# Two convolution chunks as one seven-product block, and half of the depthwise taps shared by ScalarE and VectorE

## The chip, the cores and the metric

The kernel runs on one core of a Trainium2 chip. The metric is the device time of one execution in microseconds (us). The engines are TensorE (PE, matmuls), VectorE (DVE), ScalarE (ACT), GpSimd (POOL) and SyncE (SP, which issues most transfers). Each has its own in-order instruction queue, and they synchronise by semaphores.

## The reference, cut to what matters

One decoder layer on x of 256 x 2048, in float32: a SwiGLU feed-forward part (FFN), a token mixer, a second FFN, each with a normalisation behind it. The mixer:

```python
z = h @ w_in                      # 2048 x 12288
q, k, v, u, ga, gc = split(z)     # widths 2048, 2048, 2048, 2*1024, 2048, 2048
y_attn = attention(q, k, v) @ w_attn_out
a, g = jnp.split(u, 2, axis=-1)
c = a * jax.nn.sigmoid(g)                          # 256 x 1024
c = depthwise_causal_conv(c, w_dw, 31 taps) + b_dw # per channel
y_conv = silu(layer_norm(c)) @ w_conv_out
mix = (sigmoid(ga) * y_attn + sigmoid(gc) * y_conv) @ w_out
```

## The kernel before, in words

**Arithmetic.** Each float32 matmul is made of three faster ones: activations and weights are each split into a high part (fp32r) and a low part, and high x high, high x low and low x high are added up. ScalarE writes the high part of a weight tile (`g_hi`, `w_hi`), VectorE the low part by a subtraction (`g_lo`, `w_lo`).

**Groups.** The weights of the FFNs and of `w_in` come as groups of 512 rows x 512 columns (1 MB). A group is loaded by SP into one of up to eight slots of `g_raw`, split into a ring of four (`RING`), and used by TensorE. The class `Groups` numbers groups in the order in which TensorE uses them and gives each load a slot; SP issues a load when the low part of the slot's last user is made. ScalarE's split of group n waits until TensorE has used group n-4.

**Plain and seven-product work.** The 256 rows are two tiles of 128. A plain group is used for both tiles: 24 matmuls of 512 columns. A plain chunk of 512 output columns is four groups. A seven-product block computes two chunks at once (Winograd's form of Strassen's scheme over 2 x 2 blocks of rows and inner dimension): products P1 to P7, each in two half groups a and b, so 14 product groups of 12 matmuls. Some of its weight groups are sums of loaded ones: VectorE adds them in place (T1a, T2a, T2b and so on, `add`), or a POOL transfer accumulates a group from memory onto a slot (`add_from_hbm`). Between products ScalarE copies PSUM banks (`fork`, `save_value`).

**The order of the mixing stage.** Four plain chunks for the convolution input u (gate and value of the first 512 channels, then of the second), with 33 taps of the depthwise convolution on VectorE near their end; then six `mixing_block`s, each a seven-product block for two chunks (keys and values, or gates) with four plain query groups Q1 to Q4 among it (the last for queries or a gate); attention heads of block g-1 are worked on inside block g. Then eight plain gate groups, here called gates 0 to 7. Then `attn_out`, four chunks of eight units. A unit is 256 rows x 512 columns (512 KB) with 6 matmuls for each row tile; TensorE goes through four units for the first row tile, then the same four for the second. The units come through four slots of `raw` and eight split slots (`SPLIT`). The conv and output projections follow.

**Taps.** The convolution's rows are kept transposed in `ch`, eight tiles of 128 channels x (30 + 256) positions. `taps(count)` does the next `count` steps of 248 (8 tiles x 31 taps), each a multiply-add of 128 x 256 on VectorE into `cacc`, two tiles in turn. Their places are written out by hand: 33 before the mixing blocks, 97 in them (`BLOCK_TAPS`), 8 or 6 behind each gate's low part, then 3 behind each unit's low part in `attn_out`. The second turn of the finished rows (`turn_conv_out(1)`) is behind unit 3 of the third chunk. In the last four gates VectorE also makes `oT_lo`, the low part of four attention heads, after ScalarE's `heads_hi`; the heads come back from memory (`oT`, loaded by SP behind the load of gate 3).

ScalarE's order at the gates, in which these names matter, is: split gate 0, a sigmoid of a bank, split gate 1, a sigmoid, split gate 2, two sigmoids of the banks of Q4, split gate 3, two sigmoids of `sig_c`, `heads_hi(0)`, then split gates 4 to 7 with the other `heads_hi`, with `gate_out(0)` before the split of gate 7; then the splits of units 0 to 3, `gate_out(1)`, and the other units.

## Time and profile before

| | |
|---|---|
| median of 3 runs | 2111.5 us (2111.37 to 2112.41) |
| profiled execution, first to last instruction (its span) | 2109.5 us |
| TensorE busy | 2095.7 us, 99% |
| VectorE busy | 1877.2 us, 89% |
| ScalarE busy | 1402.9 us, 67% |
| mean granted TensorE clock | 0.998 |

For the profiled execution only the span is recorded; the median of the runs lies 2.0 us above it. The span runs from the first to the last instruction, so what lies around it (start and end of the execution) is in the runs' times alone. In the rows below, a timeline row gives start, duration, engine, source line, operation, tiles and count, and in brackets the idle time before it and what ended it. A matmul's shown duration is longer than the distance from one to the next.

### The profile page before, as it was taken

What the parts mean: (1) busy time and instruction counts of PE and PEld (TensorE: products, weight loads), DVE (VectorE), ACT (ScalarE), POOL (GpSimd) and SP (SyncE); (2) the same over time, 40 slices, a digit from 0 to 9 for tenths busy, and PEclk for the clock granted to TensorE, in tenths of its full rate; (3) what the DMA queues carried; (4) which work ended last, traced back from release to release, by engine and by line L of the source; (5) the groups of instructions that cost most, each with busy time, mean ns of one, the idle gap of its engine ahead of it and who ended that gap; (6) DMA issues with size and microseconds to landing.
All of it is one profiled execution on the core that took longest, in us unless ns stands there. A gap on an engine that the chain in (4) does not pass through costs nothing.

```text
span 2109.5 us, 23778 instructions
## 1 busy us (share of the span) xinstructions
PE 2095.7 (99%) x9386; PEld 1734.6 (82%) x9386; DVE 1877.2 (89%) x1420; ACT 1402.9 (67%) x1313; POOL 216.7 (10%) x345
## 2 busy tenths in 40 slices
PE   9999999999999999999999999999999999999998
PEld 7888888888888888888888888888888888888886
DVE  7899999999996889999999986659899999999996
ACT  6677777777775546766676445335677777777773
POOL 0111111101110001011100000000111111100110
PEclk9999999999999999999999999999999999999999
DMA  9798988888985759998898556755788988899892
GB/s 369 253 295 260 279 270 266 291 300 277 289 279 231 276 158 311 299 269 270 304 301 262 212 185 240 260 178 200 244 294 255 282 272 267 290 302 278 288 285 113
DMA packets 92397, 556.65 MB, mean 264 GB/s; under 512 B 13056, under 2 KB 13440, under 8 KB 35200
## 3 DMA queue, kind: packets, MB, share of 16 engines
q1 hardware_dynamic: 68544, 437.69, 54.7%
q0 software_dynamic: 23744, 117.46, 25.8%
q8 instruction: 74, 1.21, 0.2%
q14 instruction: 35, 0.29, 0.0%
HBM read 534.13 MB, written 20.97 MB: 263 GB/s over the span
## 4 chain that ended last, share of the span: by engine, by line
PE 88%; DVE 8%; DMA 2%; ACT 1%; issue 1%; SPq 0%; DVEq 0%; ACTq 0%
PE acc L2259 14%; PE acc L2261 14%; PE acc L2260 14%; PE tb L2259 12%; PE tb L2261 12%; PE tb L2260 12%; PE acc L2197 3%; PE acc L2199 3%; PE acc L2198 3%; DVE g_lo L1338 3%; DVE cacc L1777 3%; DMA g_raw<-in_groups 1%; PE tb L2245 1%; DVE w_lo L1315 1%; DVE g_raw L1346 1%
## 5 line engine op out<-in xcount | busy, mean ns | idle before, releaser
L1338 DVE TENSOR_TENSOR g_lo<-g_raw,g_hi 128x2048 fp32r<-128x2048 f32 x506 | 1147.6, 2286 | 120.4 <-ACT g_hi L817 119.8
L817 ACT ACTIVATE g_hi<-g_raw 128x2048 fp32r<-128x2048 f32 x506 | 964.4, 1916 | 319.8 <-DVE g_raw L1346 121.5
L2259 PE MATMUL acc<-g_hi,xF_hi 128*128 128x512 f32 x1184 | 464.3, 392 | 0.6 <-ACT acc L899 0.6
L2261 PE MATMUL acc<-g_hi,xF_lo 128*128 128x512 f32 x1184 | 461.1, 389 | 0.0
L2260 PE MATMUL acc<-g_lo,xF_hi 128*128 128x512 f32 x1184 | 460.7, 389 | 0.0
L2259 PE MATMUL tb<-g_hi,xF_hi 128*128 128x512 f32 x760 | 296.3, 390 | 0.3 <-DVE g_lo L1338 0.2
L2261 PE MATMUL tb<-g_hi,xF_lo 128*128 128x512 f32 x760 | 295.7, 389 | 0.0
L2260 PE MATMUL tb<-g_lo,xF_hi 128*128 128x512 f32 x760 | 295.7, 389 | 0.0
L1346 DVE TENSOR_TENSOR g_raw<-g_raw,g_raw 128x2048 f32<-128x2048 f32 x120 | 274.3, 2286 | 1.3
L2259 PEld LDWEIGHTS acc<-g_hi,xF_hi 128*128 128x128 f32 x1184 | 222.3, 188 | 46.8 <-ACT acc L899 1.0
L2261 PEld LDWEIGHTS acc<-g_hi,xF_lo 128*128 128x128 f32 x1184 | 222.2, 188 | 46.8
L2260 PEld LDWEIGHTS acc<-g_lo,xF_hi 128*128 128x128 f32 x1184 | 222.4, 188 | 45.1
L2259 PEld LDWEIGHTS tb<-g_hi,xF_hi 128*128 128x128 f32 x760 | 142.7, 188 | 30.4 <-issue 1.1
L2261 PEld LDWEIGHTS tb<-g_hi,xF_lo 128*128 128x128 f32 x760 | 142.6, 188 | 29.8
L2102 POOL DMA_DIRECT2D g_raw<-in_groups x80 | 72.5, 941 | 918.8 <-DVE g_lo L1338 870.6
L2260 PEld LDWEIGHTS tb<-g_lo,xF_hi 128*128 128x128 f32 x760 | 142.7, 188 | 29.4
L767 ACT ACTIVATE w_hi<-raw 128x1024 fp32r<-128x1024 f32 x80 | 84.7, 1062 | 105.0 <-DMA raw<-in_stream 65.4
L2259 PE MATMUL tb<-g_hi,hT_hi 128*128 128x512 f32 x384 | 149.8, 390 | 0.0
L2261 PE MATMUL tb<-g_hi,hT_lo 128*128 128x512 f32 x384 | 149.4, 389 | 0.0
L2260 PE MATMUL tb<-g_lo,hT_hi 128*128 128x512 f32 x384 | 149.4, 389 | 0.0
L2259 PE MATMUL acc<-g_hi,hT_hi 128*128 128x512 f32 x320 | 124.7, 390 | 0.0
L2261 PE MATMUL acc<-g_hi,hT_lo 128*128 128x512 f32 x320 | 124.5, 389 | 0.0
(180 smaller groups left out, 2307.7 us busy)
## 6 DMA issues: line engine op xcount, KB each, us to landing
g_raw<-in_groups SPq DMA_DIRECT2D x356, 1024.0 KB, 7.2
g_raw<-in_groups POOLq DMA_DIRECT2D x80, 1024.0 KB, 8.6
raw<-in_stream SPq DMA_DIRECT2D x80, 512.0 KB, 4.5
bounce<-h_sq POOLq DMA_DIRECT2D x40, 256.0 KB, 5.5
h_in<-bounce POOLq DMA_DIRECT2D x160, 64.0 KB, 2.6
ln_gb<-in_ln SPq DMA_DIRECT2D x6, 1024.0 KB, 6.6
g_raw<-in_groups SPq DMA_DIRECT2D x6, 512.0 KB, 9.7
res<-in_x_rows SPq DMA_DIRECT2D x1, 2048.0 KB, 16.6
```

Source lines behind the costliest of these rows:

```text
L767: act.activation(w_hi[:, seg.split(j)], raw[:, seg.raw(j)], ACT.Copy).then_inc(hi_ready, 1)
L817: act.activation(g_hi[:, n % RING], source[:], ACT.Copy).then_inc(g_hi_ready, 1)
L1338: dve.tensor_tensor(g_lo[:, n % RING], source[:], f32(g_hi[:, n % RING]), ALU.subtract).then_inc(g_lo_ready, 1)
L1346: dve.tensor_tensor(out[:], a[:], b[:], ALU.add).then_inc(t_ready, 1)
L1777: ins = dve.scalar_tensor_tensor(out=rows if j == TAPS - 1 else cacc[:, k], in0=rows, scalar=w, in1=cacc[:, k], op0=ALU.mult, op1=ALU.add)
L2102: pool.dma_start(out=source(f, b, onto)[:].rearrange("p k n -> p (k n)"), in_=groups[k], accum_op=ALU.add).then_inc(ready, 16)
L2197: pe.matmul(out_ap, x[0][:, k, rows], w_hi[:, s, cols], start=begin, stop=False)
L2198: pe.matmul(out_ap, x[0][:, k, rows], w_lo[:, s, cols], start=False, stop=False)
L2199: return pe.matmul(out_ap, x[1][:, k, rows], w_hi[:, s, cols], start=False, stop=end)
L2259: pe.matmul(bank, x_hi_ap, g_hi[:, n % RING, blk], start=begin, stop=False, skip_group_check=True)
L2260: pe.matmul(bank, x_hi_ap, g_lo[:, n % RING, blk], start=False, stop=False, skip_group_check=True)
L2261: return pe.matmul(bank, x_lo_ap, g_hi[:, n % RING, blk], start=False, stop=end, skip_group_check=True)
```

## The change

The second pair of convolution chunks (value and gate of the second 512 channels), eight plain groups before, becomes a seven-product block of its own (`conv_pair`, numbered as block -1, `CONV`). The first mixing block begins with its query group Q1 (`FIRST_MIXING`), behind which the sigmoids read the pair's results; its product with the value moves to `conv_pair_value`. The loads are reordered to match. The 33 taps before the mixing blocks go. VectorE keeps the 124 taps of four tiles (97 in the mixing blocks as before, 4 behind each gate's low part). For the other four tiles ScalarE makes the products of row and tap (`tap_rounds`: a round is one tap of two tiles, two activations of 128 x 256), and VectorE adds two tiles at once (`shared_taps`: one add of 128 x 512 a round, none in the first round of each pair). There are 62 rounds.

```diff
-SPLIT0 = 2
+SPLIT0 = 6
+FIRST_MIXING = ("Q1", "P1a", "P1b", "Q2") + MIXING[4:]
+FIRST_MIXING_LOADS = ("Q1", "qa", "qb", "ra", "Q2", "ua", "rb", "ub", "Q3", "ga", "gb", "Q4")
+PAIR = ("P1a", "P1b", "P5a", "P5b", "P6a", "P3a", "P6b", "P3b", "P7a", "P7b", "P2a", "P2b", "P4a", "P4b")
+PAIR_LOADS = {"qa": "P4a", "ra": "P7a", "qb": "P4b", "rb": "P7b", "ua": "P3a", "ub": "P3b", "ga": "P2a", "gb": "P2b"}
+PAIR_SUMS = ("T1a", "T1b", "T2a", "T2b")
...
+TAP_ROUNDS = ((0, 1), (2, 3))
+SHARED = ((4, 5), (6, 7))
+OWN_TAPS = sum(TAPS * len(tiles) for tiles in TAP_ROUNDS)
+SHARED_ADDS = (TAPS - 1) * len(SHARED)
... SyncE
-            sp.wait_ge(conv_step, 2 + KC * TAPS)
+            sp.wait_ge(conv_step, 2 + OWN_TAPS)
+            sp.wait_ge(shared_added, SHARED_ADDS)
... ScalarE
+            def conv_pair():
+                f, g = "mix", CONV
+                split_loaded(f, g, "P1a", "qa")
+                split_loaded(f, g, "P1b", "qb")
+                split_sum(f, g, "P5a", "qa", "T1a")
+                split_sum(f, g, "P5b", "qb", "T1b")
+                fork(f, g, acc[:, BY], acc[:, BX], "P1b")
+                split_sum(f, g, "P6a", "qa", "T2a")
+                split_loaded(f, g, "P3a", "ua")
+                split_sum(f, g, "P6b", "qb", "T2b")
+                act.wait_ge(acc_out[1], 2)
+                fork(f, g, acc[:, BZ], acc[:, BW], "P5b")
+                split_loaded(f, g, "P3b", "ub")
+                conv_block(0)
+                act.wait_ge(t3a_ready, 16)
+                split(f, g, "P7a", "ra")
+                act.wait_ge(t3b_ready, fulls(f, g))
+                split(f, g, "P7b", "rb")
+                save_value(g, 0, "P6b")
+                split_loaded(f, g, "P2a", "ga")
+                save_value(g, 1, "P7b")
+                split_loaded(f, g, "P2b", "gb")
+                act.wait_ge(t4a_ready, fulls(f, g))
+                split(f, g, "P4a", "qa")
+                act.wait_ge(t4b_ready, 16)
+                split(f, g, "P4b", "qb")
...
+            def tap_rounds(rounds):
+                for r in range(products_done[0], min(products_done[0] + rounds, TAPS * len(SHARED))):
+                    j, n = r // len(SHARED), r % len(SHARED)
+                    if j == 0:
+                        act.wait_ge(o_stored, 16 * NG)
+                        act.wait_ge(ch_ready, 4)
+                    elif j > 1:
+                        act.wait_ge(shared_added, r - 2 * len(SHARED) + 1)
+                    for k, c in enumerate(SHARED[n]):
+                        w = cw[:, c * TAPS + j:c * TAPS + j + 1]
+                        if j == 0:
+                            act.activation(shared_sum[:, n, k], ch[:, c, j:j + T], ACT.Identity, scale=w,
+                                           bias=cw[:, KC * TAPS + c:KC * TAPS + c + 1]).then_inc(tap_products, 1)
+                        else:
+                            act.activation(shared_product[:, n, k], ch[:, c, j:j + T], ACT.Copy,
+                                           scale=w).then_inc(tap_products, 1)
+                products_done[0] += rounds
...
             heads_hi(0)
+            tap_rounds(6)
             for g in range(PIECES, PIECES * GATES):
                 if g % PIECES == PIECES - 1:
                     gate_out(g // PIECES - 1)
                 split_gate(g)
+                tap_rounds(4)
                 if g in HEADS_AT:
                     heads_hi(HEADS_AT.index(g))
             hi(attn_out, 0, 0, 1, 2, 3)
             gate_out(GATES - 1)
-            hi(attn_out, 0, 4, 5, 6, 7)
-            hi(attn_out, 1, *range(UD))
-            hi(attn_out, 2, *range(UD))
+            for j in range(4, UD):
+                tap_rounds(2)
+                hi(attn_out, 0, j)
... and the same for all units of chunks 1 and 2
... VectorE
+            def shared_taps(rounds):
+                for r in range(shared_done[0], min(shared_done[0] + rounds, TAPS * len(SHARED))):
+                    j, n = r // len(SHARED), r % len(SHARED)
+                    if j == 0:
+                        continue
+                    add_no = r - len(SHARED)
+                    c = SHARED[n][0]
+                    dve.wait_ge(tap_products, 2 * (r + 1))
+                    if add_no > 1:
+                        dve.wait_ge(shared_added, add_no - 1)
+                    dve.tensor_tensor(ch[:, c:c + 2, PAD:PAD + T] if j == TAPS - 1 else shared_sum[:, n], shared_sum[:, n],
+                                      shared_product[:, n], ALU.add).then_inc(shared_added, 1)
+                shared_done[0] += rounds
...
+            def conv_pair():
+                lo_group P1a; add T1a (qa += ra); lo_group P1b; add T1b (qb += rb); lo_group P5a; add T2a (qa += ua)
+                conv_value(0); lo_group P5b; add T2b (qb += ub)
+                lo_group P6a, P3a, P6b, P3b, P7a, P7b, P2a, P2b, P4a; values(g); lo_group P4b
... block 0 of mixing_block on VectorE: lo Q1, lo P1a, conv_pair_value, lo P1b, add T1a, taps, lo Q2 ...
-            lo_conv(8) ... lo_conv(15), conv_value(0), taps(11) three times
+            conv_pair()
             for g in range(PIECES * GATES):
                 lo_gate(g)
-                taps(6 if g - 1 in HEADS_AT else 8)
+                taps(4)
+                shared_taps(2 if g - 1 in HEADS_AT else 3)
                 if g - 1 in HEADS_AT:
... oT_lo of four heads
             for j in range(UD):
                 lo(attn_out, 0, j)
-                taps(3)
+                shared_taps(2)
... and the same in chunk 1 and in four units of chunk 2
... GpSimd
+            def conv_pair_sums():
+                f, g = "mix", CONV
+                pool.wait_ge(t_ready, G.sum_no[f, g, "T1a"])
+                add_from_hbm(f, g, "ra", "ua", t3a_ready)
+                pool.wait_ge(t_ready, G.sum_no[f, g, "T1b"])
+                add_from_hbm(f, g, "rb", "ub", t3b_ready)
+                pool.wait_ge(g_lo_ready, lo_count(G.at[f, g, "P6a"]))
+                add_from_hbm(f, g, "qa", "ga", t4a_ready)
+                pool.wait_ge(g_lo_ready, lo_count(G.at[f, g, "P6b"]))
+                add_from_hbm(f, g, "qb", "gb", t4b_ready)
... TensorE: conv_pair runs PAIR in order, turn_conv(0) behind P5b; block 0 begins with query_group(0, 0),
... then P1a, P1b, turn_conv(1), Q2, P5a, P5b as before
-            plain_chunk(conv + 2 * PIECES, (acc[:, 0], acc[:, 1]), after={(3, 0): lambda: turn_conv(0)})
-            plain_chunk(conv + 3 * PIECES, (acc[:, 2], acc[:, 3]))
+            conv_pair()
```

## Rows read from the trace of the kernel before

**Rows 1.** The page, busy time of each engine over the whole span.
```profile
PE 2095.7 (99%) x9386; PEld 1734.6 (82%) x9386; DVE 1877.2 (89%) x1420; ACT 1402.9 (67%) x1313; POOL 216.7 (10%) x345
```

**Rows 2.** TensorE's waits: us in total, times, longest.
```profile
PE tb L2323 <- DVE zeros L1683: 1.5, 1, 1.5
...
PE acc L2197 <- DVE sig_a L1950: 0.7, 1, 0.7
```

**Rows 3.** Groups by line and shape: busy us, mean ns of one, idle before.
```profile
L1392 DVE TENSOR_TENSOR hT_lo<-h_in,hT_hi 128x512 fp32r<-128x512 f32 x40 | 25.9, 685 | 1.6 <-ACT hT_hi L835 1.6
...
L1117 ACT ACTIVATE pr<-pr,nmax 128x256 f32<-128x256 f32 x16 | 7.9, 495 | 0.0
...
L1124 ACT ACTIVATE pT<-tb 128x384 f32<-128x384 f32 x16 | 6.8, 480 | 0.0
```

**Rows 4.** TensorE's timeline: chunk 2, P3a of block 0, gate 0, attention output.
```profile
723.11 0.39 PE L2259 MATMUL acc<-g_hi,xF_hi 128*128 128x512 f32 x1
...
794.22 0.50 PE L2259 MATMUL acc<-g_hi,xF_hi 128*128 128x512 f32 x1 [0.61 <-ACT acc L899]
...
1157.78 0.39 PE L2259 MATMUL acc<-g_hi,xF_hi 128*128 128x512 f32 x1
...
1201.30 0.39 PE L2197 MATMUL acc<-w_hi,oT_hi 128*128 128x512 f32 x1
```

**Rows 5.** VectorE's timeline in the convolution chunks and block 0.
```profile
714.55 4.49 DVE L1338 TENSOR_TENSOR g_lo<-g_raw,g_hi 128x2048 fp32r<-128x2048 f32 x2
...
746.38 0.73 DVE L1774 TENSOR_SCALAR cacc<-ch,cw 128x256 f32<-128x256 f32 x2 [7.00 <-ACT ch L1077]
...
789.44 2.28 DVE L1346 TENSOR_TENSOR g_raw<-g_raw,g_raw 128x2048 f32<-128x2048 f32 x1
```

**Rows 6.** ScalarE's timeline in block 0, the fork behind P5b.
```profile
793.59 0.58 ACT L899 ACTIVATE acc<-acc 128x512 f32<-128x512 f32 x1
```

**Rows 7.** VectorE's timeline at the gates and the first attention output units.
```profile
1153.06 3.26 DVE L1777 SCALAR_TENSOR_TENSOR cacc<-ch,cw,cacc 128x256 f32<-128x256 f32 x8
1156.23 2.30 DVE L1338 TENSOR_TENSOR g_lo<-g_raw,g_hi 128x2048 fp32r<-128x2048 f32 x1
...
1161.60 2.30 DVE L1338 TENSOR_TENSOR g_lo<-g_raw,g_hi 128x2048 fp32r<-128x2048 f32 x1
...
1176.91 1.24 DVE L1942 TENSOR_TENSOR oT_lo<-oT,oT_hi 128x1024 fp32r<-128x1024 f32 x1
...
1189.47 2.30 DVE L1338 TENSOR_TENSOR g_lo<-g_raw,g_hi 128x2048 fp32r<-128x2048 f32 x1
...
1205.62 1.22 DVE L1315 TENSOR_TENSOR w_lo<-raw,w_hi 128x1024 fp32r<-128x1024 f32 x1
```

**Rows 8.** ScalarE's timeline at the gates.
```profile
1157.98 1.09 ACT L1212 ACTIVATE sig_a<-tb 128x512 f32<-128x512 f32 x2 [2.26 <-PE tb L2261]
1158.95 1.92 ACT L817 ACTIVATE g_hi<-g_raw 128x2048 fp32r<-128x2048 f32 x1
1160.76 1.15 ACT L1249 ACTIVATE sig_c<-sig_c 128x512 f32<-128x512 f32 x2
1163.14 1.06 ACT L1218 ACTIVATE oT_hi<-oT 128x1024 fp32r<-128x1024 f32 x1 [1.23 <-DMA oT<-heads_out]
1165.62 1.92 ACT L817 ACTIVATE g_hi<-g_raw 128x2048 fp32r<-128x2048 f32 x1 [1.42 <-DMA g_raw<-in_groups]
...
1168.94 1.92 ACT L817 ACTIVATE g_hi<-g_raw 128x2048 fp32r<-128x2048 f32 x1 [0.45 <-DMA g_raw<-in_groups]
```

**Rows 9.** ScalarE's timeline, splits of units 0 and 8.
```profile
1195.36 1.06 ACT L767 ACTIVATE w_hi<-raw 128x1024 fp32r<-128x1024 f32 x1 [12.73 <-DMA raw<-in_stream]
...
1214.44 1.06 ACT L767 ACTIVATE w_hi<-raw 128x1024 fp32r<-128x1024 f32 x1 [3.03 <-DMA raw<-in_stream]
```

**Rows 10.** TensorE's timeline at the start of the kernel.
```profile
1.47 4.63 PE L2323 MATMUL tb<-zeros 128*128 128x512 f32 x10 [1.47 <-DVE zeros L1683]
5.90 1.02 PE L2313 MATMUL acc<-g_hi,xF_hi 128*128 128x512 f32 x2
```

More of the change, by code:

```diff
@@ L1134, in save_value, with conv_gate_out @@
                 fork("mix", g, act_sb[:, t], acc[:, BX], behind)
+            def conv_pair():
[24 more added lines that the diff above has]
+                split(f, g, "P4b", "qb")
+            def conv_gate_out(t):
+                act.wait_ge(g_used, mix_used(CONV, ("P2b", "P4b")[t]))
+                act.activation(k_sb[:, t], acc[:, (BY, BX)[t]], ACT.Sigmoid).then_inc(k_out, 1)
             def mixing_block(g):
@@ L1838, in queries_squared, with conv_pair_value @@
                     square(q_sq[:, :, t], act_sb[:, t], q_squared)
+            def conv_pair():
+                f, g = "mix", CONV
+                qa, qb, ra, rb, ua, ub = (source(f, g, name) for name in ("qa", "qb", "ra", "rb", "ua", "ub"))
+                lo_group(f, g, "P1a", "qa")
+                load_done(f, g, "ra")
+                split_done(f, g, "P1a")
+                add(qa, qa, ra)
+                lo_group(f, g, "P1b", "qb")
+                load_done(f, g, "rb")
+                split_done(f, g, "P1b")
+                add(qb, qb, rb)
+                lo_group(f, g, "P5a", "qa")
+                load_done(f, g, "ua")
+                split_done(f, g, "P5a")
+                add(qa, qa, ua)
+                conv_value(0)
+                lo_group(f, g, "P5b", "qb")
+                load_done(f, g, "ub")
+                split_done(f, g, "P5b")
+                add(qb, qb, ub)
+                lo_group(f, g, "P6a", "qa")
+                lo_group(f, g, "P3a", "ua")
+                lo_group(f, g, "P6b", "qb")
+                lo_group(f, g, "P3b", "ub")
+                lo_group(f, g, "P7a", "ra")
+                lo_group(f, g, "P7b", "rb")
+                lo_group(f, g, "P2a", "ga")
+                lo_group(f, g, "P2b", "gb")
+                lo_group(f, g, "P4a", "qa")
+                values(g)
+                lo_group(f, g, "P4b", "qb")
+            def conv_pair_value():
+                dve.wait_ge(k_out, TT)
+                dve.wait_ge(v_out, TT)
+                for t in range(TT):
+                    dve.tensor_tensor(act_sb[:, t], k_sb[:, t], vt[:, t], ALU.mult).then_inc(acc_out[1], 1)
             def mixing_block(g):
@@ L1964, in _ @@
                     attn_rows(1, (j // 2,))
-                taps(3)
+                shared_taps(2)
             for t in range(TT):
@@ L2569, in query_group, with conv_pair @@
                 plain_piece(G.at["mix", g, f"Q{p + 1}"], (tb[:, 2], tb[:, 3]), p)
+            def conv_pair():
+                f, g = "mix", CONV
+                X, Y, Z, W = (acc[:, bank] for bank in (BX, BY, BZ, BW))
+                pe.wait_ge(acc_out[0], 2)
+                product_group(f, g, "P1a", X, A11, 0, begin=True)
+                product_group(f, g, "P1b", X, A11, 1)
+                pe.wait_ge(x_lo, 11 + 4 * factors("mix"))
+                pe.wait_ge(acc_out[1], 2)
+                product_group(f, g, "P5a", W, S1, 0, begin=True)
+                product_group(f, g, "P5b", W, S1, 1)
+                turn_conv(0)
+                wait_fork(f, g, 0)
+                product_group(f, g, "P6a", X, S2, 0)
+                wait_fork(f, g, 1)
+                product_group(f, g, "P3a", Z, S4, 0)
+                product_group(f, g, "P6b", X, S2, 1)
+                product_group(f, g, "P3b", Z, S4, 1)
+                wait_fork(f, g, 2)
+                product_group(f, g, "P7a", X, S3, 0)
+                product_group(f, g, "P7b", X, S3, 1)
+                product_group(f, g, "P2a", Y, A12, 0)
+                product_group(f, g, "P2b", Y, A12, 1)
+                wait_fork(f, g, 3)
+                product_group(f, g, "P4a", X, A22, 0)
+                product_group(f, g, "P4b", X, A22, 1)
             def mixing_block(g):
```

157 lines of the change are left out of this document (88 added, 69 removed).

## The prediction

> **What bounds the kernel now.** I read the engine line of the page first, then TensorE's waits, then the timelines around the two edited stages. TensorE is busy 99% [rows 1], and the view of its waits has nothing longer than 1.5 us. One wait of 0.67 us behind VectorE lies in the attention output [rows 2], one of 0.61 us in block 0 [rows 4]. So only fewer matmuls, or new waits, can move the time. From the first gate matmul at 1157.78 to the first attention output matmul at 1201.30 lie 8 groups of 24 matmuls in 43.52 us [rows 4], so a matmul costs 0.2267 us: a product group (12) 2.72, a plain group (24) 5.44, a unit of the attention output (12) 2.72. Each group also needs a high part from ScalarE (1.92 [rows 8]) and a low part from VectorE (2.29, or 2.20 in a row: 4.49 for two [rows 5]). VectorE comes closest to TensorE: in a gate group it does one low part and 8 taps and starts the next 5.37 us later [rows 7], against TensorE's 5.44. It is however ahead: gate 1's low part ends at 1158.5 and is needed at 1163.2.
>
> **Part 1, the seven products.** They take 14 x 12 = 168 matmuls where the two chunks took 192: 24 x 0.2267 = -5.4 us. For VectorE 33 taps leave this stage (0.40 each in a row, 13.1 us), and 6 low parts and 4 adds come (2.20 each, 22.0). Before, VectorE had holes here, the last of 7.0 us [rows 5], so it must be laid out. Chunk 2 starts at 723.11 [rows 4], the first low part of the pair at 714.55 [rows 5]. From there to the end of block 0's T2b add, VectorE has 21 low parts and 8 adds (29 x 2.20 = 63.8), six 512-column products and subtractions (3.6), 6 taps (2.4) and 0.8 for adds that wait for the low part just issued: 70.6. One wait comes on top. Before P2b, ScalarE first copies the value bank that P7b completes, then splits: P7b's end at 752.5, 0.2 until ScalarE starts (as from 1157.78 to 1157.98 [rows 4, 8]), 0.5 for the copy and 1.95 for the split give 755.2, when VectorE has been free since 749.4: 5.8 of idle. T2b ends at 714.6 + 76.4 = 791.0, or 0.1 later where instructions don't overlap. Before, it ended at 789.44 + 2.28 = 791.7 [rows 5], and behind it came ScalarE's P6b split, the fork at 793.59 [rows 6] and TensorE's P3a at 794.22 [rows 4]. All of this comes 0.6 earlier, and TensorE's 5.4 saved are spent on waits at P5a (0.9: VectorE's conv product), P6a (0.4), P2b (2.3), P4b (0.1), and in block 0 at P5b (0.9) and P3a (1.4, where it was 0.8, and chunk 3 lost 0.3): 6.0 less the 1.1 of before. **Net -0.6.** Bounds: -6.2 (all saved, and the old wait gone too) and +1.5 (POOL's accumulating load for P4b or P5b lands late). The four added POOL loads follow adds and low parts by 15 us or more before their split is due. The moved SP loads wait for low parts at least 10 us ahead of their use, and lie beside that slack. The query group before P1a costs nothing: its 5.44 us of matmuls cover the sigmoids (0.6 each) that read the pair's banks. From block 0's P3a to the gates everything keeps its order, 0.6 earlier.
>
> **Part 2, the gates.** Here VectorE's in-order queue gets a wait it did not have. After gate 0's low part and 4 taps, `shared_taps(3)` skips rounds 0 and 1 and stands at round 2, which needs six tap products. ScalarE makes them only behind the sigmoids of Q4's banks, the split of gate 3, two sigmoids and `heads_hi(0)`, which waits for the DMA of oT: all those rows are in [rows 8]. Behind VectorE's wait stands gate 1's low part, and behind that TensorE. heads_hi started at 1163.14, now 1162.5 (the 0.6). Six products follow from 1163.5.
>
> The trace has no tap product on ScalarE. Nearest are an Exp of 128x256 with a per-partition operand, 0.495, and a copy of 128x384 without one, 0.480 [rows 3]. Less 128 columns, and overlapped by 0.1 as two sigmoids are (1.09 for two of 0.6 [rows 8]), the copy gives 0.28 each in a row, the Exp 0.40; 0.495 is the end above. I take 0.40 with 0.49 for the last, since the products carry such an operand. The Trainium skill (ScalarE: Activation LUTs, What ACT_TABLE_LOAD costs) says that each pointer operand adds about 93 ns to an activation; at 0.28 the whole sum below would be about +15, at 0.40 it is +19.6, and this trace has no pair of rows that isolates the operand.
>
> So the sixth product ends at 1166.0, the shared add (0.69, 0.60 in a row, from the 512-column row in [rows 3]) is over at 1166.6, and gate 1's low part is there at 1168.9. TensorE finished gate 0 at 1157.18 + 5.44 = 1162.6: **6.3 us idle.** Afterwards VectorE's cycle for a group is low part 2.20, 4 taps 1.6, adds 1.2 to 1.8, plus `oT_lo` 1.14 from gate 4 on: 5.6 to 6.1, more than 5.44, with no lead left. Gate 2 waits 0.6 (round 5's products wait for round 3's add). Gate 3 waits 0.8: gate 4's load starts only when gate 1's low part is done, at 1168.9, and its split, due 5.0 later as for gate 5 (1168.94 less 1163.9 [rows 7, 8]), stands before the products of rounds 6 to 9. If that load takes the 7.1 that it took before (1165.62 less 1158.5), gate 3 waits 2.8. Gates 4 to 7 wait 0.15, 0.7, 0.7, 0.3. **Sum +9.6**, bounds 6.4 and 12.5.
>
> **Part 3, the attention output.** The raw loads start behind gate 7's low part. Before, the first split came 3.6 after that (1191.8 to 1195.36 [rows 7, 9]), and TensorE needed the low part at 1201.3. Now gate 7's low part ends at 1204.8, the first unit's is there at 1210.7, and TensorE is free at 1210.2: 0.5. Unit 1 stands behind the two adds of rounds 20 and 21: 1.0. Unit 2 stands behind rounds 22 and 23, whose products ScalarE makes after four splits and `gate_out(1)`, from 1214.5 to 1216.2: low part at 1218.1, 3.6 late. Unit 3: 1.2. **Sum +6.3**, bounds 4.8 and 7.5.
>
> From unit 4 on a loop limits VectorE: low part of unit j-4, load of unit j, its split, its four products, the adds behind unit j-2. That is three units in 1.2 + 3.6 + 1.0 + 1.7 + 0.6, about 8.2 or 2.7 a unit, no faster than TensorE, so the lead does not come back at once. Units 6 and 7 meet the loads that share the queue with cgb: unit 8's split came at 1214.44, 7.6 after its slot came free at 1206.8 [rows 7, 9]. They wait 0.9 and about 2.6: **+3.5**, bounds 0 and 5. At the third chunk the wait that was 0.67 grows by **0.8** (0.3 to 2), since the last adds stand before `attn_rows(2)`. All 60 adds are done 7 us before the second turn of ch needs them.
>
> **Sum.** -0.6 + 9.6 + 6.3 + 3.5 + 0.8 = +19.6. The profiled span of 2109.5 becomes 2129.1; the median of the runs lies 2.0 above that span, so I say **2131 us**.
>
> **Rivals.** (a) Not slower: the products are ready when VectorE comes, and the change is worth its -0.6, or up to -5.4 if VectorE holds up the pair less: 2106 to 2111. It decides if six products are finished by 1159.7 (1162.6 less low part and add). Against it stands ScalarE's queue, filled to 1161.9 [rows 8] before heads_hi, even if oT lands early: then still 4.6 idle. (b) Only the first wait costs (6.3), the rest is hidden by hand-overs that overlap better than I laid them out: +5.7, 2117. For it: VectorE and ScalarE each have under 2.72 us of work per unit. Against: gates 4 to 7 are a plain sum of VectorE's work. (c) ScalarE becomes the bound in the attention output: with 0.495 a product and no overlap it has 0.97 + 1.98 = 2.95 a unit, 0.23 over TensorE for some 19 units, and 1 to 3 us more in the gates: +26, 2137. (d) TensorE's clock drops during the long idle time. At the start, the 10 matmuls from 1.47 took 4.43 us, 0.443 each, which is the 1.2 GHz level [rows 10]; some 12 at that pace cost 12 x 0.21 = 2.5 us. After the first idle time VectorE's later waits would hide them (by gate 6 the timetable has caught up), after unit 2 perhaps 1 to 2.5 would show: 2132 to 2136. The Trainium skill (TensorE: Matmul & The Clock Gate, Why this matters for your kernels) warns that an idle gap of this size drops the clock; no row here has a gap over 1.7 us inside the work, so nothing before bears on it.
>
> **Chances.** Forecast, with or without (d), 2124 to 2137: 0.62. (b) and steps to it, 2116 to 2124: 0.18. (c) and beyond, over 2137: 0.13. (a): 0.07. The range 2118 to 2140 leaves out (a), the bottom of (b) and the top of (c). A measurement of this kernel can tell 0.2% (4.2 us) from no change: faster 0.03, same 0.05, slower 0.92.
>
> **What would show it.** In the changed profile's TensorE waits: one of 5 to 7 us in gate 1 behind VectorE's low part, then several under 1, one of 3 to 4 at unit 2. On VectorE: idle time before the shared add, released by ScalarE's product, summing to over 10 us. On ScalarE: products of 0.49. In the pair: 168 matmuls, a wait at P2b, and P3a of block 0 near 793.6. Gates start within 1 us of 1157.2. Wrong would be a pair that keeps its 5 us (gates at 1153), products much above 0.5, or waits in the gates under 2 us in all.

## The result and the profile after

The changed kernel takes 2141.56 us (median of 4 runs, 2141.07 to 2143.26), the kernel before 2111.95 on the same chip (4 runs, 2111.37 to 2114.12): the ratio is 1.0138, 95% interval 1.0124 to 1.0153. So it is slower by 29.6 us, where 19.6 were forecast; 2141.56 lies just outside the range of 2118 to 2140. The profiled execution has a span of 2139.2 us, against 2109.5, with a mean granted clock of 0.994 against 0.998.

The engine line of the page, which answers to [rows 1]. TensorE executes 24 matmuls fewer and yet is busy 5.2 us longer; the slower matmuls below have a large part in that:

```profile
PE 2100.9 (98%) x9362; PEld 1734.8 (81%) x9362; DVE 1891.2 (88%) x1368; ACT 1464.3 (68%) x1447; POOL 220.2 (10%) x349
```

TensorE's waits (total, times, longest), which answer to [rows 2]. The 1.5 behind `zeros` is as before; these are the largest that are new or longer:

```profile
PE acc L2419 <- DVE g_lo L1430: 9.7, 5, 6.5
...
PE acc L2357 <- DVE sig_a L2097: 6.1, 1, 6.1
...
PE acc L2357 <- DVE w_lo L1407: 4.9, 3, 4.0
PE tb L2704 <- issue: 2.5, 2, 1.6
```

TensorE's timeline at the marks of [rows 4]: P3a of block 0, a group of attention scores, gate 0, gate 1, units 0 and 2 of the attention output, the restart behind the first turn (`turn_conv_out(0)`, TensorE's eight transposes of finished convolution rows, which stand in the second chunk), the third chunk, the restart behind the second turn:

```profile
793.82 0.50 PE L2419 MATMUL acc<-g_hi,xF_hi 128*128 128x512 f32 x1 [1.10 <-ACT acc L932]
...
918.00 0.35 PE L2704 MATMUL tb<-kT,qT 128*128 128x128 f32 x1 [1.63 <-issue]
...
1160.02 0.39 PE L2419 MATMUL acc<-g_hi,xF_hi 128*128 128x512 f32 x1
...
1172.16 0.80 PE L2419 MATMUL acc<-g_hi,xF_hi 128*128 128x512 f32 x1 [6.54 <-DVE g_lo L1430]
...
1214.38 0.47 PE L2357 MATMUL acc<-w_hi,oT_hi 128*128 128x512 f32 x1 [0.24 <-issue]
...
1222.34 0.79 PE L2357 MATMUL acc<-w_hi,oT_hi 128*128 128x512 f32 x1 [4.00 <-DVE w_lo L1407]
...
1251.00 0.48 PE L2357 MATMUL acc<-w_hi,oT_hi 128*128 128x512 f32 x1
...
1273.66 0.80 PE L2357 MATMUL acc<-w_hi,oT_hi 128*128 128x512 f32 x1 [6.06 <-DVE sig_a L2097]
...
1288.11 0.48 PE L2357 MATMUL acc<-w_hi,oT_hi 128*128 128x512 f32 x1
```

Set against the kernel before, mark by mark, this gives a ledger. The marks of before that are not in [rows 4] are 1229.29 and 1258.37 for the two restarts and 1246.56 for the third chunk, from the same view.

| mark | before | after | behind by | forecast for the stretch | measured |
|---|---|---|---|---|---|
| P3a of block 0 | 794.22 | 793.82 | -0.4 | -0.6 | -0.4 |
| gate 0 | 1157.78 | 1160.02 | +2.2 | 0 | +2.6 |
| attention output, unit 0 | 1201.30 | 1214.38 | +13.1 | +9.6 and 0.5 for unit 0 | +10.8 |
| restart behind the first turn | 1229.29 | 1251.00 | +21.7 | +5.8 and 3.5 | +8.6 |
| third chunk | 1246.56 | 1273.66 | +27.1 | +0.8 | +5.4 |
| restart behind the second turn | 1258.37 | 1288.11 | +29.7 | 0 | +2.6 |

Behind the last mark the distance stays at 29.7 to the end of the span. Three rows are off: gate 0 (the attention heads' stage), the third chunk, and the stretch behind it. The rest is within a microsecond of its forecast.

VectorE's timeline at gates 0 to 2 and at unit 2, which answers to [rows 7]:

```profile
1169.21 0.69 DVE L1873 TENSOR_TENSOR shared_sum<-shared_sum,shared_product 128x512 f32<-128x512 f32 x1 [12.25 <-ACT shared_product L1319]
...
1169.82 2.28 DVE L1430 TENSOR_TENSOR g_lo<-g_raw,g_hi 128x2048 fp32r<-128x2048 f32 x1
...
1175.26 0.69 DVE L1873 TENSOR_TENSOR shared_sum<-shared_sum,shared_product 128x512 f32<-128x512 f32 x1 [0.37 <-ACT shared_product L1319]
...
1175.87 2.29 DVE L1430 TENSOR_TENSOR g_lo<-g_raw,g_hi 128x2048 fp32r<-128x2048 f32 x1
...
1219.66 0.69 DVE L1873 TENSOR_TENSOR shared_sum<-shared_sum,shared_product 128x512 f32<-128x512 f32 x1 [3.04 <-ACT shared_product L1319]
...
1221.07 1.22 DVE L1407 TENSOR_TENSOR w_lo<-raw,w_hi 128x1024 fp32r<-128x1024 f32 x1
```

The first row is the wait that was forecast: the first shared add stands 12.25 us for ScalarE's product, and gate 1's low part (1169.82) stands behind it. From there to the next low part (1175.87) is 6.05, for one low part, 4 taps and 3 adds. The add at 1175.26 waits for the products again, since those need the add of two rounds before. The last two rows are the same picture at unit 2: 3.04 of idle time before the adds, and the low part behind them.

ScalarE's timeline at the same two places, which answers to [rows 8]:

```profile
1165.36 1.06 ACT L1285 ACTIVATE oT_hi<-oT 128x1024 fp32r<-128x1024 f32 x1 [1.22 <-DMA oT<-heads_out]
...
1166.32 0.58 ACT L1316 ACTIVATE shared_sum<-ch,cw 128x256 f32<-128x256 f32 x1
...
1168.29 0.49 ACT L1319 ACTIVATE shared_product<-ch,cw 128x256 f32<-128x256 f32 x1
...
1217.77 0.58 ACT L1273 ACTIVATE sig_c<-acc 128x512 f32<-128x512 f32 x1
...
1218.73 0.51 ACT L1319 ACTIVATE shared_product<-ch,cw 128x256 f32<-128x256 f32 x1
```

`heads_hi(0)` at 1165.36, then ten products and first terms. The four first terms (with a bias) come 0.49 apart, the products (1168.29, six in 2.56) 0.40 to 0.45 apart with 0.49 for the last. At unit 2 `gate_out(1)` (1217.77) stands ahead of the products (1218.73).

The granted clock, by the view of stretches (time, TensorE busy, its matmuls, the clock, DMA share, GB/s), behind gate 1 (two stretches), unit 2, and the third chunk (two):

```profile
1172.00:1176.00 4.00, 3.84 (x9) 0.50 0.70 244
...
1176.00:1180.00 4.00, 4.00 (x17) 0.89 0.22 53
...
1222.30:1226.00 3.70, 3.66 (x9) 0.50 0.54 155
...
1273.60:1277.00 3.40, 3.34 (x8) 0.50 0.41 134
...
1277.00:1281.00 4.00, 4.00 (x15) 0.72 0.78 256
```

The clock is at 1.2 GHz (0.50) as TensorE resumes from each of the three long waits. The matmuls are 0.43 us apart there instead of 0.2267: about 11, 13 and 13 of them.

### The profile page after: what moved, and what is told of

Read it like the earlier page. It is cut to its first block, busy times and chain, and to the rows that moved or that the text cites. A ratio compares the mean times of both kernels' runs of the same rounds, so it can differ in the third digit from the quotient of the medians.

```text
span 2139.2 us, 23891 instructions
## 1 busy us (share of the span) xinstructions
PE 2100.9 (98%) x9362; PEld 1734.8 (81%) x9362; DVE 1891.2 (88%) x1368; ACT 1464.3 (68%) x1447; POOL 220.2 (10%) x349
## 4 chain that ended last, share of the span: by engine, by line
PE 87%; DVE 6%; DMA 3%; ACT 2%; issue 1%; SPq 0%; DVEq 0%; ACTq 0%
PE acc L2419 14%; PE acc L2421 14%; PE acc L2420 14%; PE tb L2419 12%; PE tb L2421 12%; PE tb L2420 12%; DVE g_lo L1430 3%; PE acc L2357 3%; PE acc L2358 3%; PE acc L2359 3%; DMA g_raw<-in_groups 2%; DMA raw<-in_stream 1%; ACT shared_product L1319 1%; PE tb L2405 1%; DVE g_raw L1438 1%
## 5 line engine op out<-in xcount | busy, mean ns | idle before, releaser
L1430 DVE TENSOR_TENSOR g_lo<-g_raw,g_hi 128x2048 fp32r<-128x2048 f32 x512 | 1160.8, 2285 | 119.2 <-ACT g_hi L850 118.6
L850 ACT ACTIVATE g_hi<-g_raw 128x2048 fp32r<-128x2048 f32 x512 | 975.1, 1915 | 284.8 <-DVE g_raw L1438 123.3
L1438 DVE TENSOR_TENSOR g_raw<-g_raw,g_raw 128x2048 f32<-128x2048 f32 x124 | 283.3, 2285 | 1.7
L2421 PEld LDWEIGHTS tb<-g_hi,xF_lo 128*128 128x128 f32 x760 | 142.7, 188 | 29.7
```

Of the source, the lines that this page charges most:

```text
L850: act.activation(g_hi[:, n % RING], source[:], ACT.Copy).then_inc(g_hi_ready, 1)
L1430: dve.tensor_tensor(g_lo[:, n % RING], source[:], f32(g_hi[:, n % RING]), ALU.subtract).then_inc(g_lo_ready, 1)
L1438: dve.tensor_tensor(out[:], a[:], b[:], ALU.add).then_inc(t_ready, 1)
L2421: return pe.matmul(bank, x_lo_ap, g_hi[:, n % RING, blk], start=False, stop=end, skip_group_check=True)
```

## The experiments

All were compared with the kernel before on the same chip. Its medians there were 2113.8 for the first four, 2112.5 for the next four and 2112.7 for the last four, so the ratios are what compares; times in the expectations are absolute.

**1. Shared adds later in the gates.** VectorE does its own taps first and comes to the first shared add only in gate 3; ScalarE's rounds are moved to match.

```diff
... VectorE
-                taps(4)
-                shared_taps(2 if g - 1 in HEADS_AT else 3)
+                taps((8, 8, 8, 3, 0, 0, 0, 0)[g])
+                shared_taps((0, 0, 0, 5, 3, 3, 4, 4)[g])
... ScalarE
-            tap_rounds(6)
+            tap_rounds(4)
-                tap_rounds(4)
+                tap_rounds((2, 3, 3, 9)[g - PIECES])
... behind the splits of the third chunk
+            tap_rounds(2)
```

> The changed kernel with the shared adds moved later in the gates: own taps 8, 8, 8, 3 behind the first four low parts, shared rounds 5, 3, 3, 4, 4 behind the last five; ScalarE's products moved to match. Theory (the place of VectorE's wait is the cost): TensorE's waits of 6.5 us at gate 1 and of about 0.4 at the others go, the clock stays at 1.0 through the gates, the attention output starts some 10 us earlier than in the changed kernel (near 1204 instead of 1214.4), and the time is near 2131 us. The waits at unit 2 (4.0) and at the third chunk (6.1) stay. Rival (VectorE and ScalarE simply have too much work from the gates to the third chunk, wherever it stands): what is saved in the gates comes back as longer waits in the attention output, and the time stays above 2137 us.

Measured: 2129.17 (2128.66 to 2133.11), ratio 1.0079 (1.0062 to 1.0096). Gate 0 starts at 1161.77 and the attention output at 1205.29: 43.52 between them, as before. So all of the gates' loss was that wait and the crowded queue behind it. The waits at unit 2 and at the third chunk remained, the latter 0.8 longer than in the changed kernel:

```profile
1211.16 0.50 PE L2358 MATMUL acc<-w_hi,oT_hi 128*128 128x512 f32 x1 [3.00 <-DVE w_lo L1408]
...
1263.22 0.80 PE L2358 MATMUL acc<-w_hi,oT_hi 128*128 128x512 f32 x1 [6.83 <-DVE sig_a L2098]
```

**2. Plain chunks.** The kernel before with only the second half of the change: the taps shared as in the changed kernel, the two chunks plain, the 33 early places for taps empty.

```diff
-            conv_pair()
+            lo_conv(8) ... lo_conv(15), conv_value(0), as before but without taps(11) three times
... block 0 begins with P1a, as before
```

> The kernel before with the tap split alone: four plain convolution chunks, the first mixing block as before, no taps near the chunks' end, and gates and attention output as in the changed kernel. Theory (the pair is worth 0.4 us where it stands, since its 5.4 us of saved matmuls are spent on waits): about 2141 us, 0.4 over the changed kernel, or 2139 if the 2.6 us that the changed kernel lost between block 0 and the gates hang on the pair's load order. Rival (the pair's stage keeps its 5.4 us and everything is lost later): 2146 to 2147 us.

Measured: 2138.26 (2136.96 to 2139.01), ratio 1.0115 (1.0098 to 1.0132). So the pair is not what costs, and in the changed kernel it gains nothing either: P3a of block 0 starts at 792.54 here, 1.3 ahead of the changed kernel with its 24 matmuls fewer, and 1.7 ahead of the kernel before, where VectorE still has 33 taps in front of it. The three long waits are all there without the pair, and so is one at the scores:

```profile
915.61 0.35 PE L2603 MATMUL tb<-kT,qT 128*128 128x128 f32 x1 [1.80 <-issue]
...
1168.78 0.79 PE L2318 MATMUL acc<-g_hi,xF_hi 128*128 128x512 f32 x1 [6.56 <-DVE g_lo L1377]
...
1271.56 0.80 PE L2256 MATMUL acc<-w_hi,oT_hi 128*128 128x512 f32 x1 [5.05 <-DVE sig_a L2009]
```

These are the scores, gate 1 and the third chunk; unit 2 waited 4.16. The 1.80 at the scores speaks against the idea that the pair's order of loads makes them wait.

**3. P2b split first.** In the pair, ScalarE splits P2b's group before it copies the value bank that P7b completes.

```diff
-                save_value(g, 1, "P7b")
                 split_loaded(f, g, "P2b", "gb")
+                save_value(g, 1, "P7b")
```

> The changed kernel with one thing swapped: in the pair ScalarE splits P2b's weights before it copies the value bank that P7b completes. Theory: VectorE's 5.9 us of idle before P2b's low part and TensorE's wait of 2.1 there go, and so do the waits of 0.4 and 1.1 in block 0; P3a of block 0 comes near 788.6 instead of 793.8, and the time falls by about 5 us to 2136.5 us. Rival (the pair is held by VectorE's amount of work or by the accumulating loads for P4a and P4b): P3a moves by less than 2 us, the time stays at 2140 to 2142 us.

Measured: 2138.79 (2137.74 to 2140.23), ratio 1.0122 (1.0105 to 1.0139). The wait at P2b is gone, but P3a of block 0 comes only 2.8 earlier, about half of what this expected. The time alone would not show a gain: the changed kernel's second profile (11 and 12) was a run of 2137.8. The waits at P5b (0.43) and P3a of block 0 stayed; P3a:

```profile
791.05 0.50 PE L2419 MATMUL acc<-g_hi,xF_hi 128*128 128x512 f32 x1 [1.11 <-ACT acc L932]
```

VectorE now idles 3.6 us behind ScalarE's splits (1.44 before 750.62 and 2.14 before 755.05), instead of 5.9 in one piece. Removing a stall gave back the difference to the next limit, not the whole stall.

**4. Splits ahead of the products.** In the attention output ScalarE splits each unit first and makes the products after it, with two rounds already before `gate_out(1)`.

```diff
-            hi(attn_out, 0, 0, 1, 2, 3)
+            hi(attn_out, 0, 0, 1)
+            tap_rounds(2)
+            hi(attn_out, 0, 2)
+            tap_rounds(2)
+            hi(attn_out, 0, 3)
             gate_out(GATES - 1)
+            tap_rounds(2)
             for j in range(4, UD):
-                tap_rounds(2)
                 hi(attn_out, 0, j)
+                tap_rounds(2)
... and the same in chunks 1 and 2
```

> The changed kernel with ScalarE's tap products in the attention output made two units earlier: rounds 22 and 23 behind the split of unit 1, then two rounds behind each split, so that the adds behind unit j's low part need nothing that stands behind the split of unit j+2. Theory (a loop of low part, load, split, products and adds, and gate_out before the products, make the waits): the wait of 4.0 us at unit 2 falls under 1.5, the one of 6.1 at the third chunk under 2, the clock stays up after gate 1, and the time is near 2128 us. Rival (ScalarE with four products and a split, 2.57 us of the 2.72 of a unit, is the bound there): the waits shrink by less than half, the time stays above 2135 us.

Measured: 2130.78 (2129.38 to 2133.22), ratio 1.0086 (1.0069 to 1.0103). The wait at unit 2 falls from 4.00 to 0.68. The third chunk's falls to 3.25, not under 2, and eight matmuls 0.43 apart follow it. Unit 3 and the third chunk:

```profile
1218.78 0.50 PE L2362 MATMUL acc<-w_hi,oT_hi 128*128 128x512 f32 x1 [0.77 <-DVE w_lo L1412]
...
1263.00 0.50 PE L2362 MATMUL acc<-w_hi,oT_hi 128*128 128x512 f32 x1 [3.25 <-DVE sig_a L2102]
```

**5. These three together** (1, 3 and 4).

> The edits of the three experiments that each gained alone, together: shared adds only from gate 3 on, P2b's split ahead of the copy, and each unit's split ahead of the products behind it. If the costs are separate places, the gains add but for what they share: P3a of block 0 near 791.1 as in the split-first run, no wait over 1 us in the gates, waits in the attention output of 2 to 3 us in all, and still about 3 us plus some matmuls at 0.43 at the third chunk, since VectorE's order there is unchanged: attention output from 1200 to 1204, third chunk near 1252, time 2119, between 2115 and 2122. Rival, VectorE's total work is what counts and each wait removed comes back at the next place: 2125 or more.

Measured: 2117.71 (2115.53 to 2118.99), ratio 1.0023 (1.0013 to 1.0033). No gate waits over 1 us, and the attention output starts at 1200.57. The third chunk starts at 1250.69 with 3.27 of wait. The costs were separate places, and the rival (what is removed comes back) falls.

**6. Filler matmuls in the wait.** The changed kernel with 24 matmuls, whose result nothing uses, ahead of the third chunk. The expectation calls them matmuls on zeros; they are not, `fill` multiplies two parts of `xF_hi`, a tile of activations, as the row below says.

```diff
+            for m in range(24):
+                fill(tb[:, 1])
             chunk(attn_out, 2, 0, UD, 1, oT_parts, u1_attn + 2, after={(3, 1): lambda: turn_conv_out(1)})
```

> The changed kernel, with 24 matmuls on zeros (5.4 us at 0.227) ahead of the third chunk's first matmul, which waits 6.1 us there for VectorE. If the low clock behind the wait comes from the idle time, the matmuls behind it stay at 0.227 instead of 13 at 0.43, and the time falls by 2.6 us: 2139.0. Rival, the clock falls whatever TensorE does in the wait, or the fillers hold up the real ones: 2141.6 or more. What VectorE does is untouched, so the third chunk still begins near 1273.7.

Measured: 2138.75 (2137.44 to 2139.07), ratio 1.0124 (1.0107 to 1.0141), against 1.0138. The ratios alone hardly separate the two kernels, so the trace must. The fillers, the third chunk's first matmul, and the clock behind it:

```profile
1269.03 0.39 PE L2637 MATMUL tb<-xF_hi 128*128 128x512 f32 x1
...
1274.47 0.39 PE L2357 MATMUL acc<-w_hi,oT_hi 128*128 128x512 f32 x1
```

```profile
1273.60:1277.00 3.40, 3.40 (x17) 1.00 0.39 137
...
1277.00:1281.00 4.00, 4.00 (x19) 1.00 0.74 264
```

The clock is 1.00 where it was 0.50 and 0.72. From the third chunk's first matmul to the end of its first four units, where the turn starts, the changed kernel takes 13.66 us (1273.66 to 1287.32) and this one 10.89 (1274.47 to 1285.36): 2.77 less for the same 48 matmuls. VectorE was ready at 1273.7, so the fillers held the chunk up by 0.8 and 2.0 remain. The span is 2.0 shorter too, but that proves nothing, since the second profile of the changed kernel is 3.2 shorter; what shows the clock's price is the 48 matmuls.

**7. The attention rows' order.** VectorE takes the first row tile's bank two units earlier, the second's ahead of the adds. Each row tile of a chunk has its own bank, and the first is complete 5.4 us before the second.

```diff
             for j in range(4):
                 lo(attn_out, 2, j)
+                if j == 3:
+                    attn_rows(2, (1,))
                 shared_taps(2)
-            attn_rows(2)
+                if j == 1:
+                    attn_rows(2, (0,))
```

> The changed kernel with only VectorE's order at the third chunk changed: the product with the first row tile's attention rows goes behind unit 1's adds, the one with the second tile's directly behind unit 3's low part, as it is done one chunk earlier. The wait of 6.1 us at the third chunk's start goes, in its place 0.5 there and about 1.2 at the second row tile, and with no long idle time the 13 slow matmuls go too: about 7.5 us less, 2134, the restart behind the turn near 1280.6. Rival, VectorE is so far behind that TensorE then waits for the low parts of the chunk's units instead: 2138 to 2141.

Measured: 2133.1 (2131.43 to 2134.59), ratio 1.0102 (1.0085 to 1.0119). TensorE's first matmul of the third chunk, at 1266.64, is 0.14 late. VectorE's two products with the banks (`sig_a`):

```profile
1265.90 0.68 DVE L2097 TENSOR_TENSOR sig_a<-vt,acc 128x512 f32<-128x512 f32 x1
...
1270.59 0.68 DVE L2097 TENSOR_TENSOR sig_a<-vt,acc 128x512 f32<-128x512 f32 x1
```

In the changed kernel both came together at 1272.92. The 6.1 us and the slow matmuls behind them hung on the order of the bank products, the low parts and the adds in VectorE's queue.

**8. All of it, and block 0's taps later.** Experiments 5 and 7, and the six taps ahead of T2b in block 0 moved behind P3b.

```diff
-BLOCK_TAPS = ((3, 3, 1, 1, 3, 1, 1, 1, 1, 1),
+BLOCK_TAPS = ((0, 0, 1, 2, 4, 2, 2, 2, 2, 1),
```

> All three edits of the first kernel of this call, the attention rows' order of the kernel before this one, and the six taps that VectorE does in block 0 ahead of T2b moved behind P3b. The last gives VectorE 2.4 us ahead of T2b, so the waits at P5b and P3a of block 0 go (0.4 and 1.1): P3a near 789.6. At the third chunk no wait over 1 us and no slow clock. Time: 2119 less 5 less 1.5 = 2112.5, between 2109 and 2116, level with the kernel before. Rival, the heads stage or VectorE's work takes it back: 2118 or more.

Measured: 2110.33 (2109.94 to 2111.57), ratio 0.9991 (0.9982 to 1.0001), so level with the kernel before. P3a of block 0 is at 790.10. Some of what TensorE still waits for, beside the start:

```profile
PE tb L2712 <- issue: 1.9, 2, 1.1
...
PE acc L2365 <- DVE w_lo L1412: 1.4, 2, 0.8
```

**9. Fewer adds behind the first units.** Experiment 8 with one round instead of two behind units 0 to 2, made up behind unit 4 of the third chunk.

```diff
                 lo(attn_out, 0, j)
-                shared_taps(2)
+                shared_taps(1 if j < 3 else 2)
... ScalarE: tap_rounds(1) at those three places, tap_rounds(6) from unit 4 of the third chunk on
```

> The fifth-edit kernel with one shared round instead of two behind each of the attention output's first three units, and the three rounds made up behind unit 4 of the third chunk. Its last two waits of size, at units 1 and 2 (0.59 and 0.77), go: 2110.3 less 1.3 = 2109.0, below the kernel before by 0.1 to 0.2%. Rival, ScalarE can run only two rounds ahead of the adds, so its products now hold up the splits and the waits move to units 4 to 7: 2110.3 or more.

Measured: 2108.64 (2107.22 to 2112.03), ratio 0.9983 (0.9973 to 0.9992), the only one whose interval lies below the kernel before; it overlaps that of experiment 8. The waits at the units are gone from the view, and the longest left inside the work is 1.0.

**10. The same layout with plain chunks.** Experiment 2 with the edits of 1, 4 and 7.

> The two convolution chunks as plain groups, as in the kernel before, with the taps shared and laid out as in the fifth-edit kernel and its order at the third chunk. It separates the two halves of the change once nothing else waits. If the pair is worth its matmuls less what VectorE holds up (P3a of block 0 at 790.1 with the pair, about 793.3 without it), this is slower by 2 to 3 us: 2113, between 2112 and 2114. Rival, what the pair gains is lost again at the scores, which wait for the queries' transfer: level with the kernel with the pair, 2110 to 2111.

Measured: 2111.31 (2110.76 to 2114.12), ratio 0.9996 (0.9987 to 1.0005), against 0.9991 with the pair. Expected were 2 to 3 us between them, found was 1.0, and the intervals overlap. The pair's first gate is 1.5 us earlier (1155.53 against 1157.08), with waits at the scores of 1.9 in the one profile and 2.0 in the other. At P3a of block 0 the pair is 2.5 ahead (790.10 against 792.60), and 1.0 of that is lost again before the gates. So the pair's worth of 24 matmuls (5.4 us) is some 1.0 to 1.5 us in this layout, and was not separated from none.

**11 and 12. Second profiles** of the kernel before and of the changed kernel.

> The kernel before, unchanged, for a second profile of it. From P3a of block 0 to the first gate it took 363.6 us; in eight kernels with the changed order of the pair it took 364.4 to 366.6, with the same code. If those 0.8 to 3.0 us are variation from one execution to the next, this profile shows another value than 363.6 too, up to 366; if they come from the change, it shows 363.6 within 0.3.

> The changed kernel, unchanged, for a second profile of it. Up to block 0 and at gate 1, unit 2 and the third chunk it repeats (waits of 2.1, 6.5, 4.0 and 6.1 within 0.3), and the 366.2 us from P3a of block 0 to the first gate comes out between 364.3 and 366.6 if that stretch varies by itself.

Measured: one run each, 2111.62 and 2137.8. P3a of block 0 and gate 0 of the kernel before:

```profile
793.80 0.50 PE L2259 MATMUL acc<-g_hi,xF_hi 128*128 128x512 f32 x1 [0.64 <-ACT acc L899]
...
1157.61 0.39 PE L2259 MATMUL acc<-g_hi,xF_hi 128*128 128x512 f32 x1
```

The same marks of the changed kernel, and its third chunk:

```profile
793.63 0.50 PE L2419 MATMUL acc<-g_hi,xF_hi 128*128 128x512 f32 x1 [1.10 <-ACT acc L932]
...
1158.06 0.39 PE L2419 MATMUL acc<-g_hi,xF_hi 128*128 128x512 f32 x1
...
1271.54 0.80 PE L2357 MATMUL acc<-w_hi,oT_hi 128*128 128x512 f32 x1 [4.40 <-DVE sig_a L2097]
```

The stretch takes 363.8 (before; 363.6 in its first profile) and 364.4 (changed; 366.2 in its first). For the kernel before, experiment 11 had named a value within 0.3 of the first as the sign that the difference comes from the change, and it came out so. The wait at the third chunk, expected to repeat within 0.3, was 4.4 instead of 6.1; at unit 2 it was 3.5 instead of 4.0. The span was 2136.0 instead of 2139.2. So a single profile of the changed kernel can carry some 3 us that the next does not show, and differences of that size between two experiments' times say little.

## Why the prediction was wrong by 10 us

**Right.** The direction, the place of every large wait but one, and what causes them. The pair and block 0 were to come out at -0.6 and came out at -0.4: VectorE's queue spends what TensorE saves. There is some luck in that number: in experiments 1, 6 and 7, whose code up to there is the same, seven or eight slow matmuls follow the wait at P2b, and P3a of block 0 comes at 795.16, 794.65 and 794.72, which is +0.4 to +0.9. The wait at gate 1 was to be 6.3 and was 6.54. Its cause (the first shared add behind a product that stands behind `heads_hi(0)`) is shown by experiment 1, in which it is gone when the add comes later. A product was to cost 0.40 in a row and took 0.40 to 0.41; only the first four of the six that the add needs are first terms with a bias, at 0.49, so the six took 2.85 and not 2.5. Rival (c), a ScalarE that cannot keep up, falls. Unit 2 was to wait 3.6 and waited 4.0, which fell to 0.68 when the products came ahead of `gate_out(1)` (experiment 4). By the first restart the forecast was +18.8; measured were 21.7, of which 2.6 are the heads' stage. Within that sum the pieces were less good: units 3, 6 and 7 waited 0.2 in all and not 4.7, and the slow matmuls (13 at 0.43, +2.6) filled part of the place. In the second profile the later unit did wait, 1.77.

**Wrong 1: "From block 0's P3a to the gates everything keeps its order, 0.6 earlier".** The order was kept, the time was not: +2.6. The scores waited 1.63 where it was 0.79. They need the queries, which come back from memory and which ScalarE then scales; it does so 1.6 later than in the kernel before. ScalarE's timeline at that place, before and after:

```profile
915.16 1.15 ACT L1108 ACTIVATE qT<-q_sq 128x512 f32<-128x512 f32 x2 [4.04 <-DMA q_sq<-q_bounce]
...
916.75 1.15 ACT L1141 ACTIVATE qT<-q_sq 128x512 f32<-128x512 f32 x2 [4.74 <-DMA q_sq<-q_bounce]
```

Of the 2.6, 1.8 were not there in the second profile of the same kernel. Eight profiles of seven kernels with the same code from P3a to the gates lie between 364.1 and 366.6 us in this stretch, the kernel before at 363.6 and 363.8. So the changed kernel's stretch varies by 2.5 between executions, but all eight lie above both of the kernel before, by 1.8 in the mean. Experiments 2 and 10, with plain chunks, took 364.1 and 364.5. As far as these profiles tell, the term that was put at nothing is 0.3 to 3.0; why the stretch grew was not tested. The forecast should have given it a cost and a spread.

**Wrong 2: the third chunk, "grows by 0.8 (0.3 to 2)".** This is the term that failed: it grew by 5.4, and with the clock it was worth 8 us (3.7 and 5.2 in the second profile). The text said that the last adds stand before `attn_rows(2)` and priced those adds alone. It missed that VectorE arrives there with no lead. VectorE's timeline: the low part of unit 0 in the kernel before, then in the changed kernel the same low part, two adds that wait, and the first product with the banks:

```profile
1196.45 1.23 DVE L1315 TENSOR_TENSOR w_lo<-raw,w_hi 128x1024 fp32r<-128x1024 f32 x1 [1.16 <-ACT w_hi L767]
...
1213.06 1.22 DVE L1407 TENSOR_TENSOR w_lo<-raw,w_hi 128x1024 fp32r<-128x1024 f32 x1 [2.37 <-ACT w_hi L800]
...
1256.95 0.69 DVE L1873 TENSOR_TENSOR shared_sum<-shared_sum,shared_product 128x512 f32<-128x512 f32 x1 [0.50 <-ACT shared_product L1319]
...
1268.97 0.69 DVE L1873 TENSOR_TENSOR shared_sum<-shared_sum,shared_product 128x512 f32<-128x512 f32 x1 [0.86 <-ACT shared_product L1319]
...
1272.92 0.68 DVE L2097 TENSOR_TENSOR sig_a<-vt,acc 128x512 f32<-128x512 f32 x1
```

`attn_rows(2)` frees the banks that the third chunk needs from its first matmul on, but it stands behind the low parts and adds of that chunk's first four units. So VectorE must be through 20 units when TensorE is through 16. In the kernel before it started unit 0's low part 4.85 us ahead of TensorE's first matmul (1196.45 against 1201.30) and reached `attn_rows(2)` at 1245.80, just as TensorE ended the second chunk: that was the wait of 0.67, with nothing to spare. In the changed kernel it starts 1.32 ahead (1213.06 against 1214.38) and gets there at 1272.92, when TensorE has been free since 1267.4. Of the growth of 5.4, 3.5 is thus lead that was gone before the attention output began. The rest VectorE lost over TensorE on the way, where it idled behind ScalarE's products (0.50 and 0.86 here). The wait at unit 2 held up both engines and is not the cause: in experiments 4 and 5, where the products come early and that wait is nearly gone, the third chunk still waits 3.25 and 3.27.

VectorE could not win the lead back. A unit now takes 1.14 for the low part and 1.2 to 1.4 for two adds, 2.55 together, against TensorE's 2.72, which gains 0.2 a unit. The low parts of the units were made in time and hid this until then. The forecast had what it needed: its own timetable has unit 0's low part 0.5 late and says that "the lead does not come back at once", but it did not carry that to the third chunk. Experiment 7 shows that the place in the queue is what costs: with the bank's release two units earlier in the queue, the wait is gone with everything else unchanged.

**Wrong 3: the clock after a long wait.** Rival (d) had the mechanism and the size (12 matmuls, 2.5 us), and stands as shown: about 11, 13 and 13 matmuls at 0.43, and none at the third chunk in experiment 6, where TensorE was kept busy. It was counted as hidden in the gates, which it was, and as 1 to 2.5 behind unit 2. With a third long wait, which the sum did not have, it was paid again in full (2.6). This is the case that the Trainium skill (TensorE: Matmul & The Clock Gate, Why this matters for your kernels) warns of, and the trace agrees: the granted clock is 0.50 behind the waits of 6.54, 4.00 and 6.06. One row that (d) leaned on is weaker than it looked: for the start of the kernel before [rows 10], where matmuls are 0.443 apart, the view gives a granted clock of 1.00. Behind the waits distance and clock agree.

The rivals (a) and (b) fall. (b) wanted the waits behind the first to vanish, and those that the timeline shows from there to the third chunk come to 11.6 us. It was right about the small ones: gates 2 to 7 were to wait 3.25 in all, and the view shows 0.39. Slow matmuls (+2.3 behind gate 1) and short gaps took their place, so the sum of the gates came out (10.8 with unit 0, against 10.1) with other terms than the forecast's, which is luck in part.

## What to carry to other kernels

When work is split over two engines and one of them is the in-order feeder of the bound engine, put the first hand-over as late in the feeder's queue as its spare work allows; here that alone took the gates from 54.4 to 43.5 us, and with the other edits of experiments 3, 4, 7, 8 and 9 it turned 1.4% slower into 0.2% faster. Ask of every release of a bank or a slot that stands in that queue not what stands directly before it, but how far behind the queue is when it gets there; place it by when its data are ready, not by the loop's structure. In these traces a stall of 3 us or more on TensorE was paid a second time, with slow matmuls behind it, unless later waits took their place.

## What the runs showed of the hardware

The granted clock fell after waits of 3.00 and 3.25 us as well as after those of 4 to 6.5: in experiments 1 and 4 matmuls 0.43 apart followed unit 2 (from 1212.2) and the third chunk (from 1264.6), in each case beginning one to two us after the resumption. Behind the waits of 6 us they were slow from the first. The length of the wait alone does not decide it. Six profiles have the same wait of 2.10 at P2b: in the changed kernel, in its second profile and in experiment 4 no slow matmul follows, in experiments 1, 6 and 7 seven or eight do. Experiment 1 at P2b, and the granted clock behind it (TensorE busy, its matmuls, the clock, DMA share, GB/s):

```profile
757.90 0.57 PE L2420 MATMUL acc<-g_hi,xF_hi 128*128 128x512 f32 x1 [2.10 <-DVE g_lo L1431]
```

```profile
757.90:761.30 3.40, 3.40 (x9) 0.54 1.01 429
```

An activation of 128x256 with a per-partition scale takes 0.50 alone and 0.40 to 0.41 in a row, and 0.49 in a row with a per-partition bias as well. The prediction's estimate from the copy without operands [rows 3] would have been 0.28.

The stretch from P3a of block 0 to the gates, in which keys and queries go through memory and back, varied by up to 2.5 us from one profile to the next with the same code.
